# Attention stage of a two-layer diffusion backbone: from one head at a time to pairs of heads in one pipeline

## The chip, the cores and the metric

The kernel runs on one core of a Trainium2 chip. The metric is the device time of one execution in microseconds (us). Five engines work in parallel and meet only at semaphores: TensorE (PE, matrix products; PEld are its weight loads), VectorE (DVE), ScalarE (ACT), GpSimd (POOL) and SyncE (SP, which here only issues DMAs). Each engine runs its own instructions in the order in which they are written. All data is float32.

## The reference

Two layers run over a stream of 512 latent tokens and 256 context tokens of width 1024. In each layer an adaLN-modulated norm feeds one input projection, the result goes through four groups of token mixers (neighbourhood attention, a convolution, grouped-query attention, differential attention), an output projection closes it, and an expert-choice mixture of experts (16 experts) follows. The change is in the three kinds of attention:

```python
# neighbourhood attention, 4 heads of width 64: a window bias on the latent keys, then the context keys
s = jnp.concatenate([s_win.reshape(B, H, R, GRID_W, nwin), s_ctx], axis=-1)
p = softmax_f32(s).astype(v.dtype)
# grouped-query attention, 4 query heads of width 64 on 2 key heads
p = softmax_f32(jnp.einsum('bqkgd,bskd->bkgqs', qb, kk) * scale)
# differential attention, 4 heads, two softmaxes of width 32 each over one set of values
p = (p1 - lam * p2).astype(vv.dtype)
o = jnp.einsum('bhqs,bshd->bqhd', p, vv)
```

So there are 12 heads and 16 softmaxes. The latent queries see 768 keys. The context queries see the 256 context keys and are needed in layer 0 only.

## The kernel before

The whole program is one block with one instruction stream for each engine; the order of the work is the order in which the code is written, and step lists such as `P_STEPS` and `OUT_STEPS` hold it for the projections. A ring of four 2 MB slots in SBUF receives the weights. SP fills them in the order of `STREAM`, each fill waits until TensorE has released the slot, and the 96 expert blocks of a layer use eight slots (four of the ring, four more in memory that other stages have left).

**Attention.** Queries are taken in tiles of 128: four latent tiles in each layer and two context tiles in layer 0. A latent tile has 16 score units (one softmax each) and 12 heads:

- GpSimd copies the queries of each softmax into `qst`, which is zero on the partitions of the other heads (`stage`), so that a score product contracts over all 128 partitions. It also loads the bias table `bt` by its own DMA and adds the window mask to it.
- `scores(j)` on TensorE: 512 and 256 columns into two PSUM banks (L627). Three units are held at a time (`AHEAD`).
- `top(j)` on VectorE: for the bias units an add, a copy and then a maximum; for the others the maximum straight from PSUM (L1391), negated into `negmax`.
- `exp(j)` on ScalarE (L1035): exponential and row sum, into `ex`. For a differential head VectorE then forms the difference of the two (L1398 to L1402).
- TensorE transposes the probabilities, six 128-column blocks, into banks 6 and 7 (L654). VectorE copies 512 columns out (L1413) and ScalarE 256 (L1048), both to `pt`.
- TensorE multiplies: `pt` is the stationary operand and the values move, 128 columns of which 64 are used, six key tiles (L674). VectorE scales by the reciprocal of the row sum into `otok` (L1432).
- At a tile's end TensorE transposes `otok` (L613) and ScalarE writes the result into `u` (L1024, L1027).

TensorE's order for a head is: transposes of its probabilities, scores of a later unit, products with the values. Each float32 product shows as two MATMUL records in the trace, a transpose as one. In the two context tiles eight blocks of the modulation (`mod_products`, L443) lie between the heads.

Behind the attention come the norm of the differential heads (L703, L1454), the output projection (L724) and the experts (L803, L808). Behind `dn_sq`, the first step of that norm, SP starts on the first expert blocks that need the attention's memory.

## Time and profile before

| | us |
|---|---|
| median of 3 runs | 2397.31 (2393.1 to 2404.62) |
| the profiled execution | 2398.39 |
| its span | 2396.6 |
| TensorE, VectorE, ScalarE, GpSimd busy | 2149.3, 776.6, 500.7, 139.2 |
| attention of layer 0, first scores to last write of `u` | 305.1 to 586.1 |
| attention of layer 1 | 1576.5 to 1793.7 |

The page is read from the chain of work that ended last, which says which engine's work the end waits for; then by stretches, since the stages have different limits. Two DMA-heavy stretches (the experts) stand beside the two attention stretches, in which the DMA engines do nearly nothing.

### The profile page before, as it was taken

Reading aid. Unit: us, or ns where it says so; the run is one execution under the profiler, and the core shown is the slowest. Engines: PE = TensorE matmul, PEld = TensorE weight load, DVE = VectorE, ACT = ScalarE, POOL = GpSimd, SP = SyncE. Lnnn points to the kernel's source line nnn. Section 1 sums busy time; section 2 is a strip of 40 time slices with the busy share of each in tenths; the row PEclk is TensorE's granted clock in tenths of the full one; section 3 lists DMA queues with packets and bytes.
Section 4 is the critical chain, followed back from the end, with each engine's and each line's share of the span. In section 5 each row is a group of like instructions: output and inputs, shape, how many; then the busy total and the mean of one; then the engine's idle time right before and its main releaser. Section 6 shows DMA issues by size and latency. Waiting matters only on the chain.

```text
span 2396.6 us, 35456 instructions
## 1 busy us (share of the span) xinstructions
PE 2149.3 (90%) x15316; PEld 1357.1 (57%) x15316; DVE 776.6 (32%) x1328; ACT 500.7 (21%) x1072; POOL 139.2 (6%) x180
## 2 busy tenths in 40 slices
PE   6999989988986999999999499989989499988886
PEld 4656667765543666555566356556764266655553
DVE  3093566666133000000000225457662411111112
ACT  3002234432021111111111221224440211111112
POOL 0000020000000001111001000020000000000000
PEclk9999999999997999999999799989999799999999
DMA  9421230006155999999998311010002499999994
GB/s 367 161 106 36 86 156 1 0 35 247 55 226 212 368 372 375 379 364 373 380 379 311 121 57 71 36 66 1 0 10 96 167 426 426 427 427 426 427 426 196
DMA packets 44254, 526.83 MB, mean 220 GB/s; under 512 B 5328, under 2 KB 5328, under 8 KB 14032
## 3 DMA queue, kind: packets, MB, share of 16 engines
q1 hardware_dynamic: 34848, 488.52, 50.0%
q0 software_dynamic: 6960, 27.79, 3.8%
q10 hardware_dynamic: 2304, 8.39, 0.9%
q8 instruction: 118, 1.93, 0.3%
q14 instruction: 24, 0.20, 0.0%
HBM read 507.90 MB, written 16.78 MB: 219 GB/s over the span
## 4 chain that ended last, share of the span: by engine, by line
PE 65%; DMA 12%; DVE 9%; PEld 5%; issue 4%; ACT 4%; POOL 0%; ACTq 0%; DVEq 0%; SPq 0%; PEldq 0%; POOLq 0%
PE ps L803 21%; PE ps L503 10%; PE ps L808 7%; DMA u<-in_w_exp 6%; PE ps L627 6%; PE ps L674 4%; PE ps L724 4%; PE ps L654 3%; PE ps L521 2%; PE ps L897 2%; PE ps L470 2%; DMA ring<-in_w_exp 2%; PEld ps L521 1%; DMA arena<-in_w_exp 1%; PE ps L443 1%
## 5 line engine op out<-in xcount | busy, mean ns | idle before, releaser
L803 PE MATMUL ps<-ring,arena 128*64 128x256 f32 x3072 | 352.1, 386 | 16.1 <-ACT arena L1129 11.6
L803 PEld LDWEIGHTS ps<-ring,arena 128*64 128x64 f32 x3072 | 226.5, 139 | 135.4 <-issue 25.9
L803 PE MATMUL ps<-arena 128*64 128x256 f32 x2304 | 269.3, 390 | 16.4 <-DMA arena<-in_w_exp 13.7
L503 PE MATMUL ps<-u,ring 128*128 128x512 f32 (+1 forms) x800 | 277.2, 507 | 0.0
L803 PEld LDWEIGHTS ps<-arena 128*64 128x64 f32 x2304 | 169.3, 140 | 110.2 <-DMA arena<-in_w_exp 19.6
L503 PEld LDWEIGHTS ps<-u,ring 128*128 128x128 f32 x800 | 151.9, 190 | 124.2 <-issue 116.2
L627 PE MATMUL ps<-arena 128*128 128x256 f32 (+1 forms) x576 | 210.6, 487 | 8.6 <-POOL arena L1605 7.5
L1545 DVE SCALAR_TENSOR_TENSOR arena<-arena,ps 128x512 f32<-128x512 f32 x40 | 27.4, 685 | 563.8 <-ACT arena L1121 563.8
L674 PE MATMUL ps<-arena 128*128 128x128 f32 x1248 | 163.9, 279 | 22.8 <-DVE arena L1413 18.2
L674 PEld LDWEIGHTS ps<-arena 128*128 128x128 f32 x1248 | 151.2, 191 | 47.6 <-DVE arena L1413 33.9
L724 PE MATMUL ps<-u,ring 128*128 128x512 f32 (+1 forms) x384 | 145.6, 537 | 7.8 <-DVE u L1455 7.8
L627 PEld LDWEIGHTS ps<-arena 128*128 128x128 f32 x576 | 100.3, 196 | 74.1 <-issue 72.4
L1391 DVE TENSOR_REDUCE negmax<-ps 128x1 f32<-128x768 f32 (+1 forms) x128 | 105.2, 822 | 70.2 <-PE ps L627 69.1
L1035 ACT ACTIVATE arena<-ps,negmax 128x768 f32<-128x768 f32 (+1 forms) x128 | 101.7, 795 | 123.0 <-DVE negmax L1391 122.8
L521 PE MATMUL ps<-ring,u 128*128 128x256 f32 (+1 forms) x576 | 112.8, 354 | 10.3 <-ACT u L940 8.2
L1121 ACT ACTIVATE arena<-ps 128x512 f32<-128x512 f32 x40 | 23.9, 599 | 459.4 <-PE ps L803 459.4
L724 PEld LDWEIGHTS ps<-u,ring 128*128 128x128 f32 x384 | 74.1, 195 | 76.9 <-issue 64.9
L654 PE MATMUL ps<-const,arena 128*128 128x128 f32 x624 | 101.3, 283 | 17.3 <-DVEq L1404 9.0
L521 PEld LDWEIGHTS ps<-ring,u 128*128 128x128 f32 x576 | 97.0, 196 | 29.1 <-issue 15.2
L1558 DVE SCALAR_TENSOR_TENSOR h<-ps,mod,h 128x512 f32<-128x512 f32 x64 | 48.1, 751 | 178.0 <-PE ps L897 174.5
L1302 DVE SCALAR_TENSOR_TENSOR arena<-arena,small 128x798 f32<-128x798 f32 (+1 forms) x120 | 97.6, 898 | 0.0
L654 PEld LDWEIGHTS ps<-const,arena 128*128 128x128 f32 x624 | 70.6, 142 | 41.9 <-DVE arena L1432 14.4
(180 smaller groups left out, 2071.7 us busy)
## 6 DMA issues: line engine op xcount, KB each, us to landing
ring<-in_w_exp SPq DMA_DIRECT2D x96, 2048.0 KB, 16.0
arena<-in_w_exp SPq DMA_DIRECT2D x72, 2048.0 KB, 16.0
ring<-in_w_mod SPq DMA_DIRECT2D x24, 2048.0 KB, 10.5
u<-in_w_exp SPq DMA_DIRECT2D x24, 2048.0 KB, 16.7
ring<-in_w_in SPq DMA_DIRECT2D x10, 2048.0 KB, 13.3
ring<-in_w_out SPq DMA_DIRECT2D x4, 2048.0 KB, 9.5
u_rows<-arena ACTq DMA_DIRECT2D x10, 512.0 KB, 2.6
arena<-in_rpb POOLq DMA_DIRECT2D x2, 1792.0 KB, 12.5
```

What stands on the lines that cost most here:

```text
L503: mm = pe.matmul(ps[:, bb, 0:n], w[:, k, P * ct:P * ct + P], u[:, k, t0:t0 + n], start=k == 0, stop=k == KD - 1)
L521: mm = pe.matmul(ps[:, 4 + nv % 2, 0:cn], u[:, k, P * t:P * t + P], w[:, k, c0:c0 + cn], start=k == 0, stop=k == KD - 1)
L627: mm = pe.matmul(ps[:, 2 * (j % AHEAD) + c, 0:n], qst[:, SOFTMAX[j], :], qk[:, KEYS[SOFTMAX[j]], t0:t0 + n], start=True, stop=True)
L654: mm = pe.transpose(ps[:, 6 + x // 4, P * (x % 4):P * (x % 4) + P], src[:, P * x:P * x + P], cst("ident"))
L674: mm = pe.matmul(ps[:, 7, 0:P], pt[:, P * x:P * x + P], val[:, kt, v0:v0 + P], start=x == 0, stop=x == len(ktiles) - 1)
L724: mm = pe.matmul(ps[:, 4 + 2 * (i % 2) + c, 0:n], w[:, k, P * ct:P * ct + P], u[:, k, t0:t0 + n], start=k == 0, stop=k == KD - 1)
L803: mm = pe.matmul(ps[64 * c:64 * c + 64, bank, cols:cols + 256], stationary(k, i), w[i][:, k, 256 * c:256 * c + 256], start=k == 0, stop=k ...
L808: mm = pe.matmul(ps[g:g + 32, bank, cols:cols + 256], stationary(k, 2 + e), w[e][:, k, 256 * c:256 * c + 256], start=k == 0, stop=k == KD - 1,
L1035: act.activation(ex[:, j % AHEAD, 0:kn], src, ACT.Exp, bias=negmax[:, j:j + 1], accum_out=sums[:, j:j + 1]).then_inc(s["s_exp"], 1)
L1302: dve.scalar_tensor_tensor(acc[:, j, 0:n], z[:, j, bass.ds(i, n)], taps[:, j, bass.ds(i, 1)], acc[:, j, 0:n], ALU.mult, ALU.add).then_inc( ...
L1391: dve.tensor_reduce(negmax[:, j:j + 1], src, AX.X, ALU.max, negate=True).then_inc(s["s_max"], 1)
L1558: dve.scalar_tensor_tensor(h[:, dt, 0:LAT], ps[:, 6 + dt % 2, :], mod[:, l, 40 + dt, 0:1], h[:, dt, 0:LAT], ALU.mult, ALU.add).then_inc(si ...
```

## The change

**Pairs.** The unit of work becomes a pair of softmaxes: two heads of grouped-query (`"G"`) or neighbourhood attention (`"N"`), or the two softmaxes of one differential head (`"D"`). `A_PAIRS` gives eight pairs for a query tile. The host permutes columns of `w_in` and rows of `w_out` so that the two heads of a pair lie on the two partition halves of the query and the key tile. A score product then contracts over 64 partitions (32 for `"D"`) at a tile position of its own row group, with no zero-filled copy of the queries. The pair uses banks 0 to 2: unit 0 the first 768 columns, unit 1 the next.

**Softmax.** `top` copies the scores out of PSUM negated, and takes the row minimum as the accumulator of the same instruction. The bias units use a 256-column copy and a fused add and minimum over 512 columns. The exponential reads SBUF. VectorE inverts the sums, and GpSimd multiplies the probabilities by them in place, and for `"D"` also adds the two products. `ex` holds six units.

**Values.** Two heads make a quad: 12 transposes in three fills of one bank each (banks 3 to 6). ScalarE empties two of the three and VectorE one. The values are stationary (64 columns) and the probabilities move, two heads on the two column halves, into bank 7. ScalarE writes the result straight into `u`; `otok` and its transposes are gone.

**One pipeline.** All tiles of a layer, latent and context, are one list of steps for each engine, sorted by a number; there is no loop and no drain between tiles. The bias table is loaded by SP into a ring slot (slot 1 in layer 0, slot 2 in layer 1), which is released after the last bias unit; the slots of all blocks are written out in a table.

```diff
+        A_PAIRS = (("G", 0), ("D", 0), ("D", 1), ("G", 1), ("N", 0), ("D", 2), ("D", 3), ("N", 1))
...
+        def pair_at(x):
+            return 4.0 / 3.0 * x
+        def fill_at(f):
+            q, j, _ = f
+            return pair_at(q) + 4.0 / 9.0 * j
...
+        EXP_SLOTS = ((4, 5, 0, 2, 3, 1, 6, 7), (0, 4, 5, 2, 3, 1, 6, 7))
+        SLOTS = [[0, 1, 2, 3] * 4 + [0, 1] + [2, 3, 0] * 3 + [2, 3, 1, 2, 3], [0, 2, 3, 1, 0, 2, 3, 1]]
...
 TensorE
+                steps = [(p - 0.3, "scores", p) for p in range(len(at_l.pairs))]
+                steps += [(fill_at(f) + 2.1, "turn", i) for i, f in enumerate(at_l.fills)]
+                steps += [(pair_at(q) + 4.6, "values", q) for q in range(len(at_l.quads))]
+                if l == 0:
+                    steps += [(32.3 + 2 * x, "mod", x) for x in range(8)] + [(33.3 + 2 * x, "pick", x) for x in range(8)]
+                for _, what, i in sorted(steps):
+                    if what == "scores":
+                        if i:
+                            pe.wait_ge(s["s_max"], s0["units"] + 2 * i)
...
+                            cuts = [(0, LAT, TOK, LAT), (1, CTX, TOK, 2 * LAT), (0, 0, LAT, 0), (1, 0, CTX, TOK)]
...
+                            if n == 3:
+                                pe.wait_ge(s["s_half"], s0["lat"] + i + 1)
+                            mm = pe.matmul(psf[:, c0:c0 + k1 - k0], qk[r0:r0 + rn, qt, q0:q0 + P], qk[r0:r0 + rn, kt, k0:k1],
+                                           start=True, stop=True, tile_position=(r0, 0))
...
+                    elif what == "turn":
+                        pe.wait_ge(s["p_norm"], s0["heads"] + h0 + (1 if where == "lat" and j == 0 else 2))
...
+                    elif what == "values":
+                                mm = pe.matmul(ps[64 * e:64 * e + 64, 7, 0:P], val[:, kt, v0:v0 + HD], pt[:, i % N_PT, c0:c0 + P],
+                                               start=x == 0, stop=x == len(ktiles) - 1, tile_position=(0, 64 * e))
...
 ScalarE
+                steps = [(u // 2 + 0.8 + 0.05 * (u % 2), "exp", u) for u in range(2 * len(at_l.pairs))]
+                steps += [(fill_at(f) + 2.7, "turned", i) for i, f in enumerate(at_l.fills) if f[2] == "ACT"]
+                steps += [(pair_at(q) + 5.1, "out", q) for q in range(len(at_l.quads))]
...
 VectorE
+                            own(dve.tensor_scalar(dst[:, LAT:TOK], src[:, LAT:TOK], -1.0, 3.0e38, ALU.mult, ALU.min, accum_out=low))
+                            dve.tensor_tensor_reduce(dst[:, 0:LAT], src[:, 0:LAT], bt[:, 2 * g + x, off:off + LAT], -1.0, low,
+                                                     ALU.add, ALU.min, low).then_inc(s["s_max"], 1)
+                        else:
+                            dve.tensor_scalar(dst[:, 0:kn], src, -1.0, 3.0e38, ALU.mult, ALU.min,
+                                              accum_out=low).then_inc(s["s_max"], 1)
...
 GpSimd
+                    if kind == "D":
+                        pool.tensor_scalar(e0, e0, rsum[:, c0:c0 + 1], None, ALU.mult).then_inc(s["p_self"], 1)
+                        pool.tensor_scalar(e1, e1, rsum[:, c0 + 1:c0 + 2], None, ALU.mult).then_inc(s["p_self"], 1)
+                        pool.wait_ge(s["p_self"], n_self)
+                        pool.tensor_tensor(e0, e0, e1, ALU.add).then_inc(s["p_norm"], 1)
+                    else:
+                        pool.tensor_scalar(e0, e0, rsum[:, c0:c0 + 1], None, ALU.mult).then_inc(s["p_norm"], 1)
```

The order of TensorE inside a latent tile of layer 0, before. L654 are transposes of probabilities, L627 scores, L674 products with the values; "x5" means five more of the same.

```order
L654 MATMUL ps<-const,arena 128x128 [waits at_t_act,at_t_dve,at_p_diff]
L654 MATMUL ps<-const,arena 128x128 x3
L654 MATMUL ps<-const,arena 128x128 [waits at_o_ev]
L654 MATMUL ps<-const,arena 128x128
L627 MATMUL ps<-arena 128x512
L627 MATMUL ps<-arena 128x256
L674 MATMUL ps<-arena 128x128 [waits at_t_act,at_t_dve]
L674 MATMUL ps<-arena 128x128 x5
```

That is one head. The same place now, in the steady part of layer 0, from the end of one pair's scores to the end of the next but one; L651 are scores, L669 transposes, L685 products with the values.

```order
L651 MATMUL ps<-arena 128x256 [waits at_s_max]
L651 MATMUL ps<-arena 128x512 x2
L651 MATMUL ps<-arena 128x256 [waits at_s_half]
L685 MATMUL ps<-arena 64x128 [waits at_o_ev,at_t_dve,at_t_act]
L685 MATMUL ps<-arena 64x128 x11
L669 MATMUL ps<-const,arena 128x128 [waits at_p_norm,at_t_act]
L669 MATMUL ps<-const,arena 128x128 x3
L669 MATMUL ps<-const,arena 128x128 [waits at_p_norm,at_t_act]
L669 MATMUL ps<-const,arena 128x128 x3
L651 MATMUL ps<-arena 128x256 [waits at_s_max]
```

The scores wait for the maxima of the pair before, the transposes for GpSimd, and two thirds of the instructions of the values product are gone for each head. On VectorE, before, around one differential head of a latent tile (L1413 takes transposed columns out, L1391 is a maximum, L1432 scales the result):

```order
L1413 COPY arena<-ps 128x512 [waits at_t_mm]
L1398 RECIPROCAL rsum<-sums 128x2 [waits at_s_exp]
L1402 SCALAR_TENSOR_TENSOR arena<-arena,rsum 128x768 [waits at_self]
L1428 RECIPROCAL rsum<-sums 128x1 [waits at_self,at_s_exp]
L1432 TENSOR_SCALAR arena<-ps,rsum 128x64 [waits at_o_mm,at_self]
L1391 TENSOR_REDUCE negmax<-ps 128x1 [waits at_s_mm]
```

And now, a neighbourhood pair and the differential pair behind it in the first tile (L1369 and L1370 are the bias units, L1374 the others, L1397 takes transposed columns out, L1391 and L1385 are inverses):

```order
L1369 TENSOR_SCALAR arena,negmax<-ps 128x256 [waits bias_done,at_p_norm,at_s_mm]
L1370 ISA arena,negmax<-ps,ring,negmax 128x512 [waits at_self]
L1370 ISA negmax 128x1
L1397 COPY arena<-ps 128x512 [waits at_t_mm]
L1391 RECIPROCAL rsum<-sums 128x1 [waits at_s_exp] x2
L1374 TENSOR_SCALAR arena,negmax<-ps 128x768 [waits at_t_mm,at_s_mm]
L1374 TENSOR_SCALAR arena,negmax<-ps 128x768 [waits at_p_norm,at_s_mm]
L1385 RECIPROCAL rsum<-sums 128x2 [waits at_s_exp]
L1386 TENSOR_TENSOR rsum<-rsum,lam 128x1 [waits at_self]
```

The inverses of a pair stand ahead of the next pair's maxima, and those wait for transposes or for GpSimd, whose buffers they overwrite. GpSimd's own order in the first tile now is:

```order
L1544 TENSOR_TENSOR ring<-ring,const 128x3584 [waits filled1]
L1561 TENSOR_SCALAR arena<-arena,rsum 128x768 [waits at_s_rec] x2
L1555 TENSOR_SCALAR arena<-arena,rsum 128x768 [waits at_s_rec]
L1556 TENSOR_SCALAR arena<-arena,rsum 128x768
L1559 TENSOR_TENSOR arena<-arena 128x768 [waits at_p_self]
```

where before the mask stood behind ten staging copies. The mask is now first, and the multiplications are new.

## Rows read from the trace of the kernel before

**Rows 1.** The page: the chain that ended last, by engine

```profile
PE 65%; DMA 12%; DVE 9%; PEld 5%; issue 4%; ACT 4%; POOL 0%; ACTq 0%; DVEq 0%; SPq 0%; PEldq 0%; POOLq 0%
```

**Rows 2.** Stretches: us, busy PE, PEld, DVE, ACT, POOL, granted clock, DMA share, GB/s

```profile
365.00:417.00 52.00, 48.20 (x290) 36.19 (x289) 36.17 (x68) 21.34 (x47) 4.37 (x10) 1.00 0.01 1
...
512.00:587.00 75.00, 63.10 (x545) 42.42 (x544) 42.22 (x142) 22.11 (x74) 3.62 (x10) 1.00 0.55 202
```

**Rows 3.** Timeline (start, us, instructions): one head, and two tile ends

```profile
409.28 1.46 PE L627 MATMUL ps<-arena 128*128 128x512 f32 x4
...
410.58 1.50 PE L674 MATMUL ps<-arena 128*128 128x128 f32 x12
...
364.87 0.60 ACT L1024 ACTIVATE u<-ps 128x512 f32 x1 [0.56 <-PE ps L613]
416.70 0.60 ACT L1024 ACTIVATE u<-ps 128x512 f32 x1 [0.49 <-PE ps L613]
```

**Rows 4.** Groups by line and shape, 305 to 587 us: busy us, mean ns

```profile
L1391 DVE TENSOR_REDUCE negmax<-ps 128x1 f32<-128x768 f32 x48 | 45.9, 955 | 30.0 <-PE ps L627 30.0
...
L1413 DVE COPY arena<-ps 128x512 f32<-128x512 f32 x48 | 32.8, 684 | 7.0 <-PE ps L654 6.7
...
L1035 ACT ACTIVATE arena<-arena,negmax 128x768 f32<-128x768 f32 x16 | 15.0, 937 | 20.9 <-DVE negmax L1391 20.9
L1391 DVE TENSOR_REDUCE negmax<-ps 128x1 f32<-128x256 f32 x32 | 13.5, 421 | 3.7 <-PE ps L627 2.6
...
L1428 DVE RECIPROCAL rsum<-sums 128x1 f32<-128x1 f32 x48 | 7.6, 159 | 3.9 <-DVE arena L1402 2.2
...
L1035 ACT ACTIVATION_READ_ACCUMULATOR arena<-arena,negmax 128x1 f32 x16 | 3.0, 188 | 0.0
L1024 ACT ACTIVATE u<-ps 128x512 f32<-128x512 f32 x4 | 2.4, 598 | 12.0 <-PE ps L613 12.0
```

**Rows 5.** Experts of layer 0, from the chain: products on column parts

```profile
768.24 7.06 PE ps L803 x64
```

**Rows 6.** Timeline of TensorE where the tiling of the array changes

```profile
539.16 0.71 PE L674 MATMUL ps<-arena 128*128 128x128 f32 x4 [0.27 <-DVE arena L1413]
539.81 1.93 PE L443 MATMUL ps<-ring,cond_w 128*32 128x256 f32 x32
541.67 0.44 PE L654 MATMUL ps<-const,arena 128*128 128x128 f32 x2
```

**Rows 7.** GpSimd's groups over the whole trace: elementwise work

```profile
L1619 POOL TENSOR_TENSOR arena<-arena,const 128x3584 f32<-128x3584 f32 x2 | 15.5, 7749 | 10.7 <-DMA arena<-in_rpb 10.7
...
L1605 POOL COPY arena<-arena 64x256 f32 x12 | 4.7, 395 | 44.0 <-PE ps L627 43.1 <-POOL arena L1605 1.0
L1605 POOL COPY arena<-arena 64x128 f32<-64x128 f32 x16 | 4.7, 291 | 79.8 <-PE ps L627 79.0
```

**Rows 8.** Timeline: where the attention stretches begin and end

```profile
305.07 1.23 PE L627 MATMUL ps<-arena 128*128 128x512 f32 x2 [0.31 <-issue]
...
585.74 0.38 ACT L1027 ACTIVATE u<-ps 128x256 f32<-128x256 f32 x1
...
1570.36 0.69 DVE L1346 TENSOR_TENSOR arena<-arena 128x512 f32<-128x512 f32 x1
...
1576.46 2.05 PE L627 MATMUL ps<-arena 128*128 128x512 f32 x2 [7.53 <-POOL arena L1605]
...
1793.33 0.38 ACT L1027 ACTIVATE u<-ps 128x256 f32<-128x256 f32 x1
```

**Rows 9.** Timeline of SP's issues (start, us, count) behind attention of layer 1

```profile
1794.39 0.80 SPq L388 DMA_DIRECT2D arena<-in_w_exp  x2
```

**Rows 10.** Stretches, columns as in Rows 2: around a clock fall, last experts

```profile
824.90:827.50 2.60, 1.91 (x14) 1.08 (x10) 0.00 (x0) 2.37 (x6) 0.00 (x0) 1.00 1.02 359
828.00:831.50 3.50, 3.50 (x20) 2.03 (x18) 0.00 (x0) 0.00 (x0) 1.89 (x2) 0.52 1.00 431
...
2070.00:2370.00 300.00, 265.95 (x2079) 160.06 (x2080) 45.06 (x64) 33.78 (x90) 3.79 (x4) 0.99 0.97 411
```

More of the change, by code:

```diff
@@ L375, in program, with bias_table @@
+        def bias_table(l):
+            return slots[slot_of[at["bias", l]]].rearrange("p k n -> p (k n)")[:, 0:4 * BIAS_DR * GRID_W]
+        def pair_at(x):
[3 more added lines that the diff above has]
+            return pair_at(q) + 4.0 / 9.0 * j
+        MOD_LATE = range(MOD_C, MOD_C + 8)
         block = ctx.enter_context(nc.Block())
@@ new lines, in _ @@
+                n = at["bias", l]
+                pool.wait_ge(filled[slot_of[n]], 16 * (turn_of[n] + 1))
+                btv = bias_table(l).rearrange("p (m w) -> p m w", w=GRID_W)
+                pool.tensor_tensor(btv, btv, cst("mask").unsqueeze(1).to_broadcast([P, 4 * BIAS_DR, GRID_W]),
+                                   ALU.add).then_inc(sig["bias_done", l], 1)
+                at_l, s, s0 = A[l], at_sem, A[l].base
+                n_self = 2 * sum(x[0] == "D" for y in A[:l] for x in y.pairs)
```

504 lines of the change are left out of this document (214 added, 290 removed).

## The prediction

> **What bounds the kernel now.** I read the chain that ended last first: 65% of it lies on TensorE and 12% on DMA [rows 1]. Then I took the stretches, since the change touches attention alone. In a latent tile TensorE is busy 48.2 of 52 us, VectorE 36.2, ScalarE 21.3, GpSimd 4.4, and the DMA engines do nothing [rows 2]; a tile takes 416.70 - 364.87 = 51.8 us [rows 3]. So TensorE's work sets the tile, not a wait. By instruction: a score unit of 768 columns runs from 409.28 to 410.58, 1.30 us, and twelve records of 128 columns take 1.50 us, which is 0.111 us from start to start once 0.28 us of the last one's length is taken off [rows 3]. A tile has 16 units (20.8 us), 12 heads of 12 value records (16.0 us) and 78 transposed blocks (8.7 us): 45.5 us, beside 48.2 busy. Attention lasts from 305.07 to 586.12 us in layer 0 (four latent tiles, two of context with eight modulation blocks) and from 1576.46 to 1793.71 us in layer 1 [rows 8].
>
> Behind it both layers wait for it as a whole. The last experts of layer 1 keep the DMA engines 97% busy at 411 GB/s [rows 10]; does a gain get lost there? Their first blocks are issued at 1794.39, right behind attention [rows 9]. The new slot table leaves one ring slot full of experts during attention where there were two, but the slot of the bias table is free by the end, so a third block follows the two of `dn_sq` at once. All eight slots are full before the experts start, as before; the stream then starts that much earlier, and the gain of both layers passes to the end.
>
> **The change, part by part: TensorE.** *Scores.* A pair is two times 768 columns on two row groups. Nothing in this trace runs on row groups. Column groups do run beside each other: 64 records of 256 columns in 7.06 us are 0.110 us each [rows 5], where a full-width record of 256 columns needs 1.30/6 = 0.217. So a pair costs between 1.3 us (all beside each other) and 2.6 us (one after the other). The four products alternate 256, 512, 512 and 256 columns, and two wait for the half in front; I take 1.5, near the row on column groups.
> *Transposes* stay at 72 a tile, 9 a pair: 1.0 us. *Values.* A quad is 24 records of 128 columns, 2.7 us if each takes 0.111, 1.35 us by the halving that rows 5 show; I take 1.35, so 1.0 us a pair.
> *Switches.* The array now changes its tiling about three times a pair. In the trace the first of 32 records comes at 539.81, where four records at 0.111 from 539.16 end at 539.60, and the next kind starts at 541.67, where 8 groups at 0.216 end at 541.54 [rows 6]: 0.13 to 0.2 us each, 0.4 us a pair.
> The Trainium skill (TensorEngine Tiling (Array Packing), Key Properties) says that changing the tiling mode drains the engine; that speaks against weaving three modes into one stream. The trace agrees, at 0.13 to 0.2 us. Its ideal of two equal tiles (Theoretical Speedup, up to 2x) would make a pair's scores 1.3 us and the whole 12 us shorter than mine; no run here shows row tiles.
> Sum: 1.5 + 1.0 + 1.0 + 0.4 = 3.9 us a pair, 31 us a tile.
>
> **The loop around it.** PSUM holds one pair of scores, so pair p+1's scores wait for both maxima of pair p. A copy with the row minimum is bounded by the maximum on the same 768 columns, 0.955 us [rows 4], and by that plus an accumulator read as ScalarE has one, 0.19 [rows 4]; I take 1.05, the middle, so 2.1 us for two. In that time TensorE does the 2.4 us of other work, begun some 0.2 us before the maxima. Then 1.5 us of scores and 0.2 us until they can be read: 2.2 + 1.5 + 0.2 = 3.9 us, up to 4.5 where a value product and two fills lie between; 4.2 on average. The other loop is VectorE to ScalarE and back, since the inverses stand ahead of the next maxima: 1.05, two exponentials of 0.94 plus half the read of 0.19 for the sum, two inverses of 0.16 [rows 4] make 3.5 us, so it is just hidden.
> Added for each tile: two neighbourhood pairs, whose 256 and 512 columns cost 0.42 + 0.68 and two reads [rows 4], 0.45 us more each, 0.9; two fills that ScalarE must empty ahead of an exponential that is ready, with a value product before them on TensorE, 0.9 us each, 1.8; two 0.68 us copies of VectorE between a differential pair's inverse and the next maxima, 0.4 us of each not hidden, 0.8. 8 x 4.2 + 3.5 = 37.1 us a tile. ScalarE has 16 x 1.03 + 12 x 0.6 + 6 x 0.3 = 25.5 us and stays below.
>
> **GpSimd** multiplies 16 times and adds 4 times a tile. Two inputs cost 7.75 us for 3584 elements, 2.16 ns each, 1.7 us for 768; a copy costs 0.29 us at 128 and 0.40 us at 256 elements, 0.81 ns each, 0.8 us for 768 [rows 7]. A multiplication by a column is not in the trace: between 0.8 and 1.7 us; I take 1.0, near the copy, and have 22.7 us a tile. At 1.7 the tile has 34 us, still below 37, but a differential pair then takes 5.1 us, and the transposes that free `ex` for the pair two further on wait for it twice a tile: 3.5 + 5.1 + 0.6 = 9.2 against 8.4 us, 1.6 us a tile, 13 us in all.
> The skill (GPSIMD Engine Reference, Engine selection) would leave elementwise work to VectorE, as GpSimd is about 2x slower for two inputs and roughly at line rate for one. The trace agrees for the add (2.16 ns), and by the page the multiplication lies at the copy's end, where I have it.
>
> **Context.** A pair has 256 columns each way: two maxima of 0.42 [rows 4], two exponentials of 0.6, inverses 0.3, and half a copy make 2.3 us; every second pair has a modulation product of 1.93 us [rows 6] ahead of its scores, about 0.9 more. 2.75 us a pair, 44 us for 16; the bounds are 2.0 and the present 4.3 (69 us over 16). The eight blocks have three slots instead of four. A block is asked for four pairs (11 us) ahead, and 202 GB/s in this stretch [rows 2] are 2 MB in 10 us, so it just comes in time.
>
> **Sum.** Layer 0 starts as before. First maxima at 307.3, 4 x 37.1 = 148.4, context 44 less its last 2.75, then 5.5 us until the last output: 502.4 instead of 586.1, 83.7 us less. In layer 1 the staging copies go, which hold the first scores from 1571.05 to 1576.46 [rows 8]: 5.4 us, in the sum below. First maxima at 1574, 31 steps of 4.64 are 143.8, then exponentials, GpSimd, last transposes and values, 10 us: 1727.8 instead of 1793.7, 65.9 us less. The bias table costs nothing: it is asked for before attention begins, and the first bias pair comes four pairs or 17 us into it, which covers its landing and the mask of 7.75 us [rows 7]; without that cover its price is the 8 us once. Together 149.6 us: 2398.4 - 149.6 = 2248.8 by the profiled execution, which stands 1.1 us above the median, so **2248 us**.
>
> **The rivals.** *Row groups run one after the other.* For it: no row shows row groups. Against it: column groups reach full overlap. Scores of 2.6 us make the loop 5.0 to 5.6 us and hide the ScalarE delays: 44.4 us a tile, 58 us more, 2306 us.
> *GpSimd is the bound.* For it: 16 multiplications and 4 adds are 20 large operations on an engine that has four such in the whole trace. If one takes 2.5 us, above both bounds, the tile has 16 x 2.5 + 6.6 = 46.6 us: 76 us more, 2324 us. Above 2.8 us each, attention gains nothing in the latent tiles.
> *The clock falls, and the kernel gets slower.* From 824.9 to 827.5 TensorE did only transposes with gaps, and its clock was 0.52 in the next 3.5 us [rows 10]. The new stream is nearly a quarter transposes and waits for three engines. At the lower level (1.2 GHz) the 3.9 us of work in a pair become 7.6, and the tile with its waits 64 us: 12 us more than before in each of eight tiles, no gain in context, 2490 us. It decides once more than about two thirds of the latent stretch runs at that level. Against it: full clock in the present tiles with 48 of 52 us busy, and 0.99 in the last experts with 266 of 300 [rows 2, 10]; I expect about 85% busy.
> *The pairs bring no gain.* The loop with a single PSUM set could be so ragged that it lasts over 50 us a tile; no price that I found gives it.
>
> **Chances.** Forecast 0.73, serial row groups 0.10, GpSimd 0.11, clock 0.04, no gain 0.02. Less than 0.5% (12 us) can't be told from no change here. Faster: 0.73 + 0.10 + 0.11 = 0.94, the same 0.01, slower 0.05. The range: with scores at 1.3 us, no delays of fills and copies and 2.2 us for a context pair, 2205; the two next rivals at 2306 and 2324. I take 2198 to 2325.
>
> **What would show it.** Right: a latent tile of 35 to 39 us with PE busy 80 to 90% at full clock; the score records of a pair (L651) starting within 0.1 us of each other on the two halves and spanning 1.3 to 1.6 us; value records (L685) in twos; GpSimd's multiplication between 0.8 and 1.3 us; first scores of layer 1 within 1 us of the last rotary add; context near 44 us; the experts' stretches as long as before. Wrong: scores of 2.6 us; transposes (L669) that wait for GpSimd; a granted clock below 0.95 in the tiles; a tile above 42 or below 32 us.

## The result, and the profile after

The changed kernel takes 2311.08 us (median of 4 runs, 2308.88 to 2312.51); beside it the kernel before takes 2395.2 us (4 runs, 2390.55 to 2404.62). The ratio is 0.9643, with a 95% interval of 0.9612 to 0.9675. The forecast was 2248 us. So the gain is real, 84 us of the 149.6 that were worked out. The profiled run took 2312.19 us, its span is 2310.1 us.

First, of the page of the changed kernel, the chain that ended last, by engine:

```profile
PE 63%; DMA 10%; POOL 9%; DVE 6%; ACT 4%; PEld 4%; issue 3%; ACTq 0%; SPq 0%; DVEq 0%; PEldq 0%; POOLq 0%
```

GpSimd had 0% of this chain before [rows 1] and has 9% now. Then the stretches, with the columns of [rows 2]: a latent tile, and the context with the end of attention.

```profile
349.50:392.50 43.00, 31.94 (x280) 25.04 (x280) 22.61 (x62) 23.12 (x50) 42.13 (x20) 0.96 0.01 2
...
485.00:540.00 55.00, 48.43 (x530) 31.07 (x524) 23.20 (x112) 25.09 (x85) 33.75 (x39) 0.94 0.75 273
```

TensorE fell from 48.2 to 31.9 us a tile, GpSimd rose from 4.4 to 42.1 of 43 us. The tile fell from 51.8 to between 42.6 and 47.2 us (a tile of the changed kernel and of the experiments is read from its first exponential to the first of the next). The groups by line and shape, 302 to 540 us, which answer to [rows 4, 7]:

```profile
L1561 POOL TENSOR_SCALAR arena<-arena,rsum 128x768 f32<-128x768 f32 x32 | 70.1, 2207 | 0.2
L1021 ACT ACTIVATE arena<-arena,negmax 128x768 f32<-128x768 f32 x64 | 59.3, 928 | 59.7 <-DVE arena L1374 30.5 <-DVE negmax L1370 28.4
L669 PE MATMUL ps<-const,arena 128*128 128x128 f32 x336 | 53.8, 302 | 37.5 <-POOL arena L1559 36.5 <-POOL arena L1561 1.0
...
L1374 DVE TENSOR_SCALAR_CACHE_REDUCE arena<-ps 128x768 f32<-128x768 f32 x48 | 44.0, 953 | 26.4 <-PE ps L669 13.2 <-PE ps L651 13.2
...
L1559 POOL TENSOR_TENSOR arena<-arena 128x768 f32<-128x768 f32 x16 | 28.9, 1807 | 1.3
...
L1544 POOL TENSOR_TENSOR ring<-ring,const 128x3584 f32<-128x3584 f32 x1 | 7.8, 7757 | 244.6 <-DMA ring<-in_rpb 244.6
```

GpSimd's multiplication takes 2.21 us, not the 1.0 of the sum and not within its bounds of 0.8 to 1.7, and the engine is idle 0.2 us ahead of 32 of them. TensorE's transposes (L669) wait 36.5 us for its sums of differential pairs. The maximum with its copy is 0.95 us and 0.08 for the read, 1.03 against the 1.05 taken. Then the timeline of one place (start, us), which answers to [rows 3, 5]: scores of a pair, values of a quad.

```profile
400.26 1.56 PE L651 MATMUL ps<-arena 32*128 32x256 f32 x8 [0.49 <-DVE arena L1374]
...
401.75 1.53 PE L685 MATMUL ps<-arena 128*64 128x128 f32 x24
```

A pair's scores take 1.56 us against 1.5 forecast, a quad's values 1.53 against 1.35. Where attention begins and ends, which answers to [rows 8, 9]:

```profile
301.88 1.56 PE L651 MATMUL ps<-arena 64*128 64x256 f32 x8 [0.35 <-DVE mod L1196]
...
538.83 0.28 ACT L1035 ACTIVATE u<-ps 128x128 f32<-128x128 f32 x1 [0.84 <-PE ps L685]
...
1518.29 0.69 DVE L1315 TENSOR_TENSOR arena<-arena 128x512 f32<-128x512 f32 x1
1519.10 1.34 PEld L651 LDWEIGHTS ps<-arena 64*128 64x128 f32 x8 [3.06 <-issue]
...
1706.95 0.28 ACT L1035 ACTIVATE u<-ps 128x128 f32<-128x128 f32 x1 [1.71 <-PE ps L685]
1707.91 0.81 SPq L412 DMA_DIRECT2D arena<-in_w_exp  x2
```

| | before | forecast | after |
|---|---|---|---|
| attention of layer 0, from its first scores | 281.0 | 197.3 | 237.2 |
| from there to the last rotary add of layer 1 | 984.9 | 984.9 | 979.9 |
| from there to the end of its attention | 222.7 | 156.7 | 188.3 |

The first scores of layer 0 came 3.2 us earlier as well (301.88 against 305.07 [rows 8]). Against the forecast that is +39.9 - 3.2 - 5.0 + 31.6 = 63.3 us, and the profiled run stands 2312.2 - 2248.8 = 63.4 us above it. Behind the attention of layer 1 both kernels take 602.9 us to the end of the span, so the gain passes through the experts' stream, as the prediction had it. The stretches of a single execution are less sure than the whole: between the two attentions, runs below whose code is the same there take from 973.8 (e1_short) to 985.3 us (e8_mask).

Why GpSimd and TensorE wait for each other is seen in half a tile of the changed kernel. GpSimd's rows, then TensorE's (start, us):

```profile
401.84 2.21 POOL L1555 TENSOR_SCALAR arena<-arena,rsum 128x768 f32<-128x768 f32 x1 [0.57 <-DVE rsum L1386]
404.03 2.20 POOL L1556 TENSOR_SCALAR arena<-arena,rsum 128x768 f32<-128x768 f32 x1
406.31 1.81 POOL L1559 TENSOR_TENSOR arena<-arena 128x768 f32<-128x768 f32 x1
408.25 2.21 POOL L1555 TENSOR_SCALAR arena<-arena,rsum 128x768 f32<-128x768 f32 x1
410.43 2.21 POOL L1556 TENSOR_SCALAR arena<-arena,rsum 128x768 f32<-128x768 f32 x1
412.71 1.80 POOL L1559 TENSOR_TENSOR arena<-arena 128x768 f32<-128x768 f32 x1
414.49 8.90 POOL L1561 TENSOR_SCALAR arena<-arena,rsum 128x768 f32<-128x768 f32 x4
423.58 2.21 POOL L1555 TENSOR_SCALAR arena<-arena,rsum 128x768 f32<-128x768 f32 x1 [0.19 <-DVE rsum L1386]
```

```profile
414.66 1.94 PE L669 MATMUL ps<-const,arena 128*128 128x128 f32 x8 [3.14 <-POOL arena L1559]
416.53 2.02 PE L685 MATMUL ps<-arena 128*64 128x128 f32 x24
418.48 1.56 PE L651 MATMUL ps<-arena 32*128 32x256 f32 x8
```

VectorE's maxima of the pair in between wait for the same transposes:

```profile
415.87 0.42 DVE L1369 TENSOR_SCALAR_CACHE_REDUCE arena<-ps 128x256 f32<-128x256 f32 x1 [4.67 <-PE ps L669]
```

There are two limits here, and they lie side by side. GpSimd's own work fills the half tile: 12.7 us for two differential pairs in a row and 8.9 us for four other multiplications. But there is a chain too: TensorE's transposes of the second differential pair wait until 414.51, the next scores stand behind them, and from there it is 9.1 us over scores, maxima, exponentials and reciprocal to the next differential pair's first multiplication at 423.58. 12.7 + 9.1 is 21.7 us as well. The chain leaves the transposes on two ways that end within 0.3 us of each other: VectorE's maxima, whose buffer the transposes free (they end at 418.23), and TensorE's own order (the scores at 418.48). The experiments take the sum and the chain apart.

### The profile page after: what moved, and what is told of

It reads as the page before. It is cut to its first block, busy times and chain, and to the rows that moved or that the text cites. A ratio compares the mean times of both kernels' runs of the same rounds, so it can differ in the third digit from the quotient of the medians.

```text
span 2310.1 us, 34889 instructions
## 1 busy us (share of the span) xinstructions
PE 2017.5 (87%) x15256; PEld 1269.2 (55%) x15256; DVE 654.3 (28%) x1262; ACT 520.8 (23%) x1118; POOL 487.8 (21%) x274
## 4 chain that ended last, share of the span: by engine, by line
PE 63%; DMA 10%; POOL 9%; DVE 6%; ACT 4%; PEld 4%; issue 3%; ACTq 0%; SPq 0%; DVEq 0%; PEldq 0%; POOLq 0%
PE ps L801 21%; PE ps L531 11%; PE ps L806 7%; PE ps L722 6%; DMA u<-in_w_exp 4%; PE ps L549 3%; DMA ring<-in_w_exp 3%; POOL arena L1555 2%; POOL arena L1556 2%; PE ps L685 2%; PE ps L895 2%; POOL arena L1561 2%; PEld ps L801 2%; PE ps L651 2%; POOL arena L1559 2%
## 5 line engine op out<-in xcount | busy, mean ns | idle before, releaser
L1561 POOL TENSOR_SCALAR arena<-arena,rsum 128x768 f32<-128x768 f32 (+1 forms) x80 | 154.9, 1951 | 103.9 <-DVE rsum L1391 103.3
L1021 ACT ACTIVATE arena<-arena,negmax 128x768 f32<-128x768 f32 (+1 forms) x160 | 134.4, 842 | 122.6 <-DVE arena L1374 64.3
L669 PE MATMUL ps<-const,arena 128*128 128x128 f32 x624 | 99.6, 305 | 70.6 <-POOL arena L1559 69.5
L651 PE MATMUL ps<-arena 64*128 64x256 f32 (+3 forms) x576 | 124.6, 550 | 30.2 <-DVE arena L1374 18.0
L669 PEld LDWEIGHTS ps<-const,arena 128*128 128x128 f32 x624 | 75.9, 155 | 98.7 <-issue 94.0
L1374 DVE TENSOR_SCALAR_CACHE_REDUCE arena<-ps 128x768 f32<-128x768 f32 (+1 forms) x128 | 100.3, 820 | 67.8 <-PE ps L651 37.5
L1590 POOL DMA_INDIRECT y_rows<-u,add_l x16 | 23.2, 1451 | 444.2 <-ACT u L1113 371.6
L1578 POOL DMA_INDIRECT arena<-u_rows,rows_l x18 | 17.7, 984 | 463.5 <-PE ps L784 397.2
L549 PEld LDWEIGHTS ps<-ring,u 128*128 128x128 f32 x576 | 98.0, 197 | 29.5 <-issue 15.2
L651 PEld LDWEIGHTS ps<-arena 64*128 64x128 f32 (+1 forms) x576 | 78.1, 204 | 60.8 <-DVE arena L1374 28.2
L1544 POOL TENSOR_TENSOR ring<-ring,const 128x3584 f32<-128x3584 f32 x2 | 36.7, 18352 | 305.3 <-DMA ring<-in_rpb 305.3
```

Of the source, the lines that this page charges most:

```text
L549: mm = pe.matmul(ps[:, 4 + nv % 2, 0:cn], u[:, k, P * t:P * t + P], w[:, k, c0:c0 + cn], start=k == 0, stop=k == KD - 1)
L651: mm = pe.matmul(psf[:, c0:c0 + k1 - k0], qk[r0:r0 + rn, qt, q0:q0 + P], qk[r0:r0 + rn, kt, k0:k1], start=True, stop=True, tile_position=( ...
L669: mm = pe.transpose(ps[:, 3 + i % 4, P * x:P * x + P], ex[:, (2 * p + e) % N_EX, P * (y % n):P * (y % n) + P], cst("ident"))
L1021: act.activation(ex[:, i % N_EX, 0:kn], ex[:, i % N_EX, 0:kn], ACT.Exp, scale=-1.0, bias=negmax[:, i % 16:i % 16 + 1], accum_out=sums[:, i ...
L1374: dve.tensor_scalar(dst[:, 0:kn], src, -1.0, 3.0e38, ALU.mult, ALU.min, accum_out=low).then_inc(s["s_max"], 1)
L1561: pool.tensor_scalar(e0, e0, rsum[:, c0:c0 + 1], None, ALU.mult).then_inc(s["p_norm"], 1)
```

## The experiments

Each ran with the kernel before on the same chip. A time is a median of 4 runs with its ratio to the kernel before, or a single time where no ratio stands.

**Is it GpSimd at all?** e1_short:

```diff
-                    kn = TOK if where == "lat" else CTX
+                    kn = P
```

> GpSimd's 20 operations a latent tile (and its operations in the context tiles) work on 128 columns instead of 768 (256): most probabilities stay unnormalised, everything else is as it was. Theory (GpSimd's 16 x 2.21 + 4 x 1.81 = 42.6 us of work is what a tile of 43.5 us waits for): GpSimd falls to about 20 x 0.6 = 12 us, the tile to what the loop over PSUM allows, 37 us (35 to 39), eight tiles give 50 us, the mask's 3.9 us at the start of layer 0 stop counting, the context loses 2 to 8 us; 2250 us (2240 to 2265), and the granted clock in the tiles goes back above 0.95. Rival (the loop over the one PSUM set, or TensorE at its lower clock, is what holds the tile, and GpSimd is only busy beside it): the tile stays at 42 to 44 us, 2300 to 2311 us.

Measured: 2208.48 us, ratio 0.9218 (0.9189 to 0.9247). Its second and third tile:

```profile
341.90:374.90 33.00, 30.47 (x280) 23.75 (x280) 21.31 (x65) 23.00 (x51) 11.36 (x20) 1.00 0.01 1
374.90:407.90 33.00, 30.47 (x280) 23.74 (x280) 21.31 (x65) 23.00 (x51) 11.37 (x20) 1.00 0.00 1
```

The rival falls: without GpSimd's load the tile loses 10 us and the clock is full. But the tile is 33.0 us, not 37, and the time is 42 us below the theory's: the loop that the prediction set at 37.1 us is no longer than 33.0. TensorE is busy 30.5 of 33.0 us, where the sum had 31.

**Another form of the same multiplication.** e2_bcast:

```diff
-                        pool.tensor_scalar(e0, e0, rsum[:, c0:c0 + 1], None, ALU.mult).then_inc(s["p_norm"], 1)
+                        pool.tensor_tensor(e0, e0, rsum[:, c0:c0 + 1].to_broadcast([P, kn]), ALU.mult).then_inc(s["p_norm"], 1)
```

and likewise for the two multiplications of a differential pair.

> The multiplication by a column is written as an operation with two inputs, the second one the reciprocal read again and again along the row; nothing is left out. Theory: if it costs what the addition costs (1.81 us for 768 columns, against 2.21), GpSimd has 20 x 1.81 = 36.2 us a tile, the tile comes down to 37 to 38 us, 45 us less in all, 2266 us (2255 to 2280). If the repeated read costs more (2.2 us), no change, 2311 us. Rival (loop or clock holds the tile): 2300 to 2311 us whatever the multiplication costs.

Measured: 2234.31 us, ratio 0.9317 (0.9293 to 0.9341), tiles of 35.8 us. Its groups on GpSimd:

```profile
L1561 POOL TENSOR_TENSOR arena<-arena,rsum 128x768 f32<-128x768 f32 x64 | 92.5, 1466 | 113.2 <-DVE rsum L1391 113.2
L1559 POOL TENSOR_TENSOR arena<-arena 128x768 f32<-128x768 f32 x32 | 57.9, 1809 | 2.5
```

A column read again and again costs 1.47 us, a third less than the operation made for a column, and less than the 1.81 that was expected, so the tile and the time fell below the range expected. The new form alone is worth 77 us against the changed kernel.

**What GpSimd charges for.** e4_forms and e9_chain give one form to each latent tile; the edit is a choice of the operation by layer and tile.

> One form of GpSimd's multiplication for each latent tile, the additions as they are (values are not the reference's where the column is left out). Layer 0: tile 0 by a constant, tile 1 two inputs with the column repeated, tile 2 a copy in place, tile 3 two inputs of full width. Layer 1: tile 0 as it was, tile 1 all on 128 columns, tile 2 all on 384 columns, tile 3 as it was. Theory: a duration per form (column 2.21 as seen; constant 2.2 if the arithmetic costs and 0.8 if the column does; two inputs 1.81; copy 0.8), and each tile as long as GpSimd's sum or 37 us, whichever is more: with a constant at 2.2 43 us, two inputs 37 to 38, copy 37, 384 columns 37 (20 x 1.2 = 24 us of work), as it was 43.5. Rival (loop or clock): all tiles 42 to 44 us, whatever the form.

Measured: 2258.93 us. The multiplication (mean of one), and the tile that it stands in: by a constant 2.13 us (tile of 44.8, with the mask), repeated column 1.47 (35.8), copy 0.83 (33.3), the tile by itself 1.47 (35.7), on 384 columns 33.4 us, on 128 columns 33.0 us. Two of its copies and the sum behind them:

```profile
391.69 1.60 POOL L1566 COPY arena<-arena 128x768 f32<-128x768 f32 x2 [2.78 <-DVE rsum L1386]
393.37 1.82 POOL L1577 TENSOR_TENSOR arena<-arena 128x768 f32<-128x768 f32 x1
```

The tile follows the duration down to 33 us. With multiplications of 0.8 us, inside the prediction's bounds, it is 33.3 us.

**Less work for GpSimd, given to ScalarE.** e3_act, and the same with another place in ScalarE's order, e6_act2:

```diff
+                        act.activation(e1, e1, ACT.Copy, scale=rsum[:, c:c + 1]).then_inc(s["a_norm"], 1)
...
+                steps += [(p + 1.45, "scale", p) for p, x in at_l.heads if on_act(at_l.pairs[p][0], x)]
```

In e6_act2 the step stands at p + 0.97.

> The second head of each pair of grouped-query or neighbourhood attention (4 of 16 multiplications a tile, 4 of 16 in a context tile) is multiplied by ScalarE, a copy with the reciprocal as its scale, behind the second exponential of the pair; nothing is left out. Theory: GpSimd has 12 x 2.21 + 4 x 1.81 = 33.8 us a tile, ScalarE 23.1 + 3.7 = 26.8, the tile falls to the loop's 37 to 38.5 us, 2268 us (2255 to 2280). Rival (loop or clock holds the tile): no gain, or a loss of up to 4 us a tile if the multiplication delays the next exponential: 2305 to 2340 us.

> As e3_act (GpSimd's multiplication in its first form, 2.21 us, the second head of a G or N pair on ScalarE), but ScalarE's multiplication stands right behind the second exponential and ahead of the copies of transposed columns. Theory of e3_act's loss (its multiplication stood behind a copy that waits for transposes, which wait for GpSimd, so GpSimd's queue was not filled: it idled 14 us of 47.6 in a tile): with the new place the tile is the larger of GpSimd's 33.8 us and the loop, 34 to 38 us, 2215 to 2260 us. Rival (the work on ScalarE itself is what costs, wherever it stands): 46 to 49 us a tile, 2320 to 2340 us.

Measured: e3_act 2330.25 us, ratio 0.9724 (0.9697 to 0.975), 19 us slower than the changed kernel, tiles of 43.5 to 48.7 us; e6_act2 2304.35 us, tiles of 41.9 to 43.8. Neither kept the theory's number, although both take 8.8 us a tile from GpSimd: e3_act came out at its rival, e6_act2 between its theory and its rival. The place matters: in e3_act the multiplication runs behind a copy that waited 3.62 us, and the next exponential starts at 405.17, 1.4 us behind its maximum (0.96 us from 402.82). TensorE's granted clock in e3_act is also down, 0.86 and 0.78 in its second and third tile; how much of the loss is the clock was not taken apart.

```profile
403.85 0.60 ACT L1041 ACTIVATE arena<-ps 128x512 f32<-128x512 f32 x1 [3.62 <-PE ps L680]
404.35 0.93 ACT L1047 ACTIVATE arena<-arena,rsum 128x768 f32<-128x768 f32 x1
405.17 0.92 ACT L1033 ACTIVATE arena<-arena,negmax 128x768 f32<-128x768 f32 x1
```

But the sum of GpSimd's work (33.5 us) no longer explains a tile of 42 us. In e6_act2 GpSimd is idle in places, and its half tile from 400.21 to 422.04 is 12.7 us of two differential pairs and 9.1 us until the next:

```profile
400.21 2.21 POOL L1574 TENSOR_SCALAR arena<-arena,rsum 128x768 f32<-128x768 f32 x1 [3.61 <-DVE rsum L1403]
...
411.09 1.80 POOL L1578 TENSOR_TENSOR arena<-arena 128x768 f32<-128x768 f32 x1
412.87 2.21 POOL L1580 TENSOR_SCALAR arena<-arena,rsum 128x768 f32<-128x768 f32 x1
417.33 2.21 POOL L1580 TENSOR_SCALAR arena<-arena,rsum 128x768 f32<-128x768 f32 x1 [2.26 <-DVE rsum L1408]
422.04 2.21 POOL L1574 TENSOR_SCALAR arena<-arena,rsum 128x768 f32<-128x768 f32 x1 [2.51 <-DVE rsum L1403]
```

**Sum or chain.** e9_chain; in layer 1 it cuts by the kind of pair, in layer 0 it gives each tile another form:

```diff
+                    if form in ((1, 0), (1, 1)) and kind != "D" or form in ((1, 2), (1, 3)) and kind == "D":
+                        kn = P
```

> GpSimd's operations cut to 128 columns by kind, and other forms (values are not the reference's). Layer 1, tiles 0 and 1: the multiplications of G and N pairs cut, those and the addition of D pairs full (4 x 6.2 + 8 x 0.6 = 29.7 us of GpSimd a tile). Tiles 2 and 3: D cut, G and N full (8 x 2.21 + 4 x 1.7 = 24.5 us). Layer 0, all full: tile 0 multiplies as an addition of the tile to itself, tile 1 ends a D pair with a product of the two units instead of their sum, tile 2 adds a constant, tile 3 adds the repeated column. Theory of the chain (what e6_act2 showed: the two D pairs in a row take 12.6 us on GpSimd, then transposes, the next pair's maxima and exponentials take some 9 us until the next D pair is there, 21.8 us for half a tile, whatever else GpSimd does): tile 1 of layer 1 stays at 41 to 43.5 us, tiles 2 and 3 fall to 33 to 34. Rival (the sum of GpSimd's work): all of them at 33 to 35 us. Forms: an addition of two inputs 1.8 us and a product 1.45 if the operation sets it, both 1.8 (or 1.45) if the operands do.

Measured: 2266.93 us. Tile 1 of layer 1, with the multiplications of the other pairs cut, and tile 2, with those of the differential pairs cut:

```profile
1543.90:1587.80 43.90, 33.56 (x290) 26.12 (x287) 24.08 (x65) 23.30 (x52) 29.49 (x20) 0.94 0.00 1
1587.80:1620.80 33.00, 30.46 (x280) 23.74 (x280) 21.31 (x63) 23.00 (x52) 23.09 (x20) 1.00 0.01 1
```

43.9 us with 29.5 of GpSimd work, 33.0 with 23.1: the chain through the differential pairs holds the tile, whatever else GpSimd has to do. That decides against the plain sum. Of the forms: adding the tile to itself takes 1.47 us, a product of two different tiles 1.81, so the second operand sets the price and not the operation.

**Which link of the chain.** e10_ring8 and e12_later, both on e6_act2. The first edit is in both, the second in e12_later alone, which also has the copies and outputs one pair later:

```diff
-N_EX, N_PT = 6, 3
+N_EX, N_PT = 8, 2
```

```diff
-                steps += [(fill_at(f) + 2.1, "turn", i) for i, f in enumerate(at_l.fills)]
-                steps += [(pair_at(q) + 4.6, "values", q) for q in range(len(at_l.quads))]
+                steps += [(fill_at(f) + 3.1, "turn", i) for i, f in enumerate(at_l.fills)]
+                steps += [(pair_at(q) + 5.6, "values", q) for q in range(len(at_l.quads))]
```

> As e6_act2 (42.0 to 43.8 us a tile with 33.5 us of GpSimd), with eight buffers for the probabilities instead of six, the memory taken from the third buffer of transposed columns; nothing is left out. Theory of the chain: the maxima of the pair behind the two D pairs need no longer wait for the first transposes behind them, GpSimd gets its next work during the D pairs, and the tile falls to 34 to 37 us, 2225 to 2255 us. Rival (not the chain but TensorE's order of steps holds it, or two buffers of transposed columns are too few): 41 to 44 us a tile, 2295 to 2320 us.

> e10_ring8 (GpSimd's first form of the multiplication, 33.5 us a tile; 40.7 us a tile; eight buffers), with everything behind GpSimd one pair later in the order of TensorE, VectorE and ScalarE: transposes 3.1 instead of 2.1 pairs behind the scores, copies, values and output likewise. In e10_ring8 the half tile of 20.3 us is the two D pairs on GpSimd (12.7 us) and 7.7 us from there, over TensorE's transposes, which the next scores stand behind, to the next D pair's reciprocal. Theory of the chain through TensorE's order: with one more pair between, the scores no longer stand behind the wait, and the tile falls to 34 to 36.5 us, GpSimd's 33.5 us and little more; 2235 to 2260 us. Rival (something else, such as ScalarE's work in line, holds it at 40.7 us): no change, 2285 to 2295 us.

Measured: e10_ring8 2289.88 us, tiles of 40.5 to 44.3 us, far above its theory and close to its rival. The buffers were not the only link. The maxima that waited 4.67 us for the transposes now stand right behind their own scores (at 403.10), but TensorE still waits with its next scores behind it.

```profile
406.16 1.06 PE L681 MATMUL ps<-const,arena 128*128 128x128 f32 x8 [3.11 <-issue]
407.16 1.53 PE L697 MATMUL ps<-arena 128*64 128x128 f32 x24
408.62 1.56 PE L660 MATMUL ps<-arena 32*128 32x256 f32 x8
```

e12_later 2225.15 us, ratio 0.9287 (0.9243 to 0.9331), 65 us less than e10_ring8 by the order of steps alone, with tiles of 33.4 to 33.8 us behind each layer's first. The later order with six buffers was not run. Its stretch of 34 us:

```profile
379.00:413.00 34.00, 30.78 (x290) 23.98 (x288) 21.55 (x63) 26.67 (x55) 33.67 (x17) 1.00 0.01 1
```

GpSimd is busy 33.7 of 34 us: now, and only now, its sum is the bound. The theory that failed for e6_act2 and e10_ring8 holds once TensorE's next scores stand ahead of the wait. e10_ring8, whose granted clock is 1.00 from 352 to 430 us, also shows what a lower clock does: the same 8 transposes behind the wait take 1.94 us in the changed kernel and 1.06 in e10_ring8, the values 2.02 and 1.53. The chain's second part is 9.1 us there and 7.7 here. That difference of 1.4 us belongs to the clock and to the two added buffers together, since the maxima's way through the buffers is gone in e10_ring8 too.

**Both ends shortened.** e5_dact and e11_ring8d:

```diff
+                        pool.tensor_tensor(e0, e0, rsum[:, c0:c0 + 1].to_broadcast([P, kn]), ALU.mult).then_inc(s["p_self"], 1)
...
+                        pool.wait_ge(s["a_norm"], n_self)
+                        pool.tensor_tensor(e0, e0, e1, ALU.add).then_inc(s["p_norm"], 1)
...
+                        act.activation(e1, e1, ACT.Copy, scale=rsum[:, c:c + 1]).then_inc(s["a_norm"], 1)
```

> GpSimd multiplies with the repeated column (1.47 us, as e2_bcast showed) and the second product of each differential pair is made by ScalarE; nothing is left out. Theory: what is left of GpSimd in e2_bcast (35.8 us a tile against 33.0 with short operations) is the chain of two differential pairs in a row, 2 x 4.75 us on GpSimd against 2 x 4.1 of the loop; with 3.3 us a pair the tile falls to 33.0 to 33.5 us, the context by 0 to 2 us, and the time from 2234 to 2210 us (2205 to 2220). Rival (ScalarE's added 0.93 us delays the exponentials or the copies of transposed columns, as it may have in e3_act): 36 to 38 us a tile, 2235 to 2255 us.

> As e5_dact (GpSimd 24.6 us a tile, TensorE busy 30.3 of 33.2 us), with eight buffers for the probabilities and two for the transposed columns; nothing is left out. Theory: here GpSimd's chain is already short, the tile is held by TensorE and the loop over the one PSUM set, and two more buffers bring nothing: 33.0 to 33.4 us a tile, 2207 to 2214 us. Rival (the buffers hold it still): 31 to 32 us a tile, 2195 to 2203 us; or the missing third buffer of transposed columns costs: over 34 us a tile, above 2215 us.

Measured: e5_dact 2210.86 us, ratio 0.9242 (0.921 to 0.9273), tiles of 33.2 us, as expected; e11_ring8d 2208.05 us, ratio 0.9213 (0.9181 to 0.9244), tiles of 32.3, between its theory and its rival. Both beat the kernel before by 7.6 to 7.9% and the changed one by 100 us or more; that eight buffers bring 0.9 us a tile is seen in the traces, but the two intervals overlap.

**Are the row groups side by side?** e7_serial, on e1_short:

```diff
-                            cuts = [(0, LAT, TOK, LAT), (1, CTX, TOK, 2 * LAT), (0, 0, LAT, 0), (1, 0, CTX, TOK)]
+                            cuts = [(0, LAT, TOK, LAT), (0, 0, LAT, 0), (1, CTX, TOK, 2 * LAT), (1, 0, CTX, TOK)]
...
-                            if n == 3:
+                            if n == 2:
```

> On the kernel with GpSimd's short operations (e1_short, 33.0 us a tile): the four score products of a latent pair in the order of the units, and the second unit's wait until the first unit's are done, so that the two row groups never work at once; leaves the same normalisation out. Theory (the two row groups run side by side, 1.56 us a pair, and TensorE is nearly the bound): 2.6 to 2.8 us a pair, tile 33.0 + 8 x 1.1 = 42 us, the first maximum of a pair can start earlier, which takes back up to 0.9 us a pair, so 35 to 42 us; 2225 to 2280 us. Rival (the row groups share one stream anyway): scores still 1.6 us a pair, tile 33, 2208 us.

Measured: 2355.37 us, tiles of 48.1 us. A pair, from its timeline:

```profile
383.45 3.17 PE L651 MATMUL ps<-arena 64*128 64x256 f32 x8
```

Side by side they are, 1.56 against 3.17 us. The time lies far above the range expected: the two halves in turn cost more than 2 x 1.3 us, which is 8 x 1.6 = 12.9 of the 15.1 us that the tile gains in length, and the earlier first maximum gives nothing back. The rest goes with a granted clock of 0.93, at which some values products take 2.2 to 2.6 us instead of 1.53. The first tile of each layer is longer still, 57.4 and 58.5 us; in layer 0 its granted clock is 0.67.

**The mask.** e8_mask cuts it to 256 columns in layer 0.

> The changed kernel with the mask of the bias table of layer 0 added to 256 of 3584 columns only (the rest is left out). Theory (the mask, 7.76 us on GpSimd from 301.8, keeps the first multiplication from 305.7 to 309.6, and since GpSimd is the bound this is not made up): GpSimd's first multiplication starts 3.9 us earlier against the first scores, and the attention of layer 0 is 3.9 us shorter, 233.3 us instead of 237.2; 2307 us. Rival (covered, as the prediction had it): attention of layer 0 as long as before, within 1 us.

Measured: 2308.14 us; layer 0's attention takes 233.0 us against 237.2. GpSimd's first multiplication starts 4.1 us behind the first scores instead of 7.7, and GpSimd now waits for the first reciprocal:

```profile
304.45 0.72 POOL L1545 TENSOR_TENSOR ring<-ring,const 128x256 f32<-128x256 f32 x1 [245.06 <-DMA ring<-in_rpb]
308.54 4.39 POOL L1562 TENSOR_SCALAR arena<-arena,rsum 128x768 f32<-128x768 f32 x2 [3.36 <-DVE rsum L1391]
```

The earlier start is shown, the shorter attention is not. Layer 1, whose mask is whole in both kernels, takes 182.5 us in this run (first scores at 1522.94, last write ends at 1705.41) and 188.1 in the changed kernel, so one execution differs from another by more than the 4.2 us. TensorE's granted clock in layer 1's first tile is 0.91 here and 0.82 there.

## Why the prediction was right, and where its mechanism was not

The time of 2311 us lies in the stated range of 2198 to 2325, but near its upper end, which two rivals had set, and in part by luck: an error of about 100 us and one of about 40 lie against each other. What was named as the sign of being right mostly did not come (a tile of 35 to 39 us, GpSimd's multiplication of 0.8 to 1.3 us, context near 44 us); the scores side by side, the staging gone and the unchanged experts did. Three of the four signs of being wrong came: transposes that wait for GpSimd, a granted clock below 0.95, tiles above 42 us.

- *TensorE's work.* Right. Scores 1.56 us a pair (1.5), values 1.53 us a quad (1.35), transposes with a switch 1.06 for eight; 30.5 us a tile where the granted clock is 1.00, against 31. e7_serial shows that running the halves side by side is worth 1.6 us a pair. The text on the change says that two thirds of the instructions of the values product are gone; they are not: the traces have 1248 records before (L674) and 1248 after (L685). What fell is their time, from 18.2 to about 10 us a tile, since two heads run beside each other.
- *GpSimd.* The step that failed is the price of its multiplication: "A multiplication by a column is not in the trace: between 0.8 and 1.7 us; I take 1.0, near the copy". It takes 2.21 us. The upper bound was taken from an operation with two inputs, as if one input had to be cheaper; it isn't. The rival with GpSimd as the bound had 46.6 us a tile at 2.5 us each, and 2324 us; at 2.21 it is 42.6, and 42.6 to 47.2 came. That rival, which had a chance of 0.11, is what happened, with the mechanism incomplete; the forecast's own case, with a chance of 0.73 and the loop over PSUM as the bound, did not come.
- *The wait behind GpSimd.* The prediction priced it at 1.6 us a tile for a multiplication of 1.7 us, by the transposes that free `ex`. That wait is in the trace (4.67 us at 415.87). But e10_ring8 shows that taking it away alone leaves tiles above 40 us, and e12_later that TensorE's order is a second way of the same chain, which the prediction lacks: the transposes of the second differential pair stand ahead of the next scores. At 2.21 us this chain is as long as GpSimd's sum.
- *The loop of 37.1 us.* Wrong the other way. With GpSimd cut short the tile is 33.0 us, below even the 8 x 4.2 = 33.6 us without the 3.5 us added for neighbourhood pairs, fills and copies. So two errors lie against each other: GpSimd's price is worth 2311 - 2208 = 103 us, the loop and smaller terms 2248 - 2208 = 40 us. With 1.0 us a multiplication the changed kernel would have come out near 2210 us, not at 2248; this is an estimate from e1_short and from the tile of 33.3 us with copies of 0.83 us in e4_forms.
- *The context.* From its first exponential to the last write 57.9 us in the changed kernel and 50.5 in e1_short; the forecast had 46.7 from the first maxima. So some 4 us are there without GpSimd's load and 7 come with it. GpSimd still works on the last latent tile until 483.8 us, 2.5 us into the context, and its multiplications on 256 columns take 0.93 us; the two were not taken apart.
- *The bias table costs nothing.* The reason given does not hold: its mask stands ahead of GpSimd's first multiplication and holds it up by 3.6 us (e8_mask). That the first pair with a bias comes later was the wrong cover to look at, since the engine's order puts the mask before every multiplication. Whether the 3.6 us reach the time is not shown.
- *Clock.* I expected full clock. The granted clock is 0.76 and 0.82 in the first tile of layers 0 and 1 and 0.86 to 0.98 in the others, and 0.77 where TensorE is busy 1.3 of 4 us:

```profile
412.00:416.00 4.00, 1.34 (x7) 1.37 (x8) 0.13 (x1) 0.00 (x0) 3.92 (x3) 0.77 0.00 0
```

  It feeds back, since TensorE's part of the chain runs slower. The waits alone do not explain it: in the later tiles it is 1.00 in e1_short and e12_later, which do not have them, but also in e10_ring8 (352 to 430 us), where the transposes still wait 3.1 us; and the first tile of layer 0 is low without them too (0.90 in e1_short, 0.78 in e12_later). What decides it is open.
- *The rest.* The first scores of layer 1 come 0.1 us behind the last rotary add, so the staging's 5.4 us went. The 5.0 us between the layers were not forecast, and they lie within what that stretch differs by from one execution to another (973.8 to 985.3 us with the same code there), so they may be no gain at all.

## What to carry to other kernels

An operation that the trace does not show has no upper bound from one that looks dearer; where the whole forecast hangs on GpSimd, price each form by itself, since the same product takes 1.47 or 2.21 us by how it is written. And before work is given to an engine, ask what stands behind the instruction that will wait for it: a sum that fits (33.5 us in a tile of 33.6) is kept only if the next round's first step is queued ahead of the wait and has a free buffer to go to. Two slow pieces in a row count as a latency of 12.7 us, not as an average of 6.
